# Fifteen Strassen pairs in the MLP instead of fourteen, with a new order of the last corners

## The reference

```python
ff = jnp.square(jax.nn.relu(x @ w_ff1)) @ w_ff2          # hidden width 4096
x  = layer_norm(ALPHA * x + ff, ln3_g, ln3_b)            # over the 1024 columns of a token
```

## Time and profile before

| | |
|---|---|
| median of 3 runs | 396.94 us (396.78 to 397.25) |
| the profiled execution | 396.8 us |
| its span, first to last instruction | 394.9 us |
| TensorE busy | 387.3 us (98%), 2090 matmuls |
| VectorE busy | 343.2 us (87%) |
| ScalarE busy | 258.5 us (65%) |
| POOL busy | 77.4 us (20%) |

### The profile page before, as it was taken

One profiled execution on the slowest core, in us unless ns is written; L12 is line 12 of the kernel. 1 busy time (PEld: TensorE's weight loads), 2 busy tenths in 40 slices (PEclk: granted clock), 3 DMA queues, 4 the chain that ended last, 5 costly groups with the idle time before them and its releaser, 6 DMA issues.

```text
span 394.9 us, 5646 instructions
## 1 busy us (share of the span) xinstructions
PE 387.3 (98%) x2090; PEld 331.7 (84%) x2090; DVE 343.2 (87%) x445; ACT 258.5 (65%) x344; POOL 77.4 (20%) x75
## 2 busy tenths in 40 slices
PE   8999999999999999999999999999999999999993
PEld 6888888888988888889988888888888888888882
DVE  5599595899988786969667899999999999999796
ACT  6666568756554638447645578777888888888720
POOL 2049400037870205000005300000000000000000
PEclk9999999999999999999999999999999999999999
DMA  8997737743656181563536449787677778776002
GB/s 292 373 378 269 248 107 250 259 159 113 224 195 215 63 300 65 212 214 116 205 135 209 135 145 305 218 245 227 210 242 217 230 234 243 231 235 218 0 2 106
DMA packets 25026, 79.44 MB, mean 201 GB/s; under 512 B 1735, under 2 KB 3111, under 8 KB 20903
## 3 DMA queue, kind: packets, MB, share of 16 engines
q1 hardware_dynamic: 22592, 75.24, 54.6%
q0 software_dynamic: 2016, 3.67, 5.4%
q10 hardware_dynamic: 390, 0.17, 0.2%
HBM read 78.02 MB, written 1.05 MB: 200 GB/s over the span
## 4 chain that ended last, share of the span: by engine, by line
PE 97%; DMA 1%; DVE 1%; issue 0%; DVEq 0%; ACT 0%
PE bank L1633 17%; PE bank L1634 17%; PE bank L1635 17%; PE bank L2018 13%; PE bank L1692 13%; PE bank L1696 7%; PE bank L2025 7%; PE bank L1844 2%; PE bank L1639 1%; DMA raw<-in_lead 1%; PE bank L1798 1%; PE bank L1831 0%; PE bank L1897 0%; PE bank L1946 0%; PE bank L1790 0%; PE bank L1789 0%
## 5 line engine op out<-in xcount | busy, mean ns | idle before, releaser
L1045 DVE TENSOR_TENSOR w_lo<-raw,w_hi 128x2048 fp32r<-128x2048 f32 x30 | 70.6, 2359 | 6.0 <-ACT w_hi L622 5.8
L622 ACT CAST w_hi<-raw 128x2048 fp32r<-128x2048 f32 x32 | 60.7, 1912 | 11.2 <-PE bank L1635 9.3
L2018 PE MATMUL bank<-actA,w_hi 128*128 128x512 f32 x224 | 55.4, 390 | 0.0
L2018 PEld LDWEIGHTS bank<-actA,w_hi 128*128 128x128 f32 x224 | 42.0, 188 | 8.7
L592 POOL DMA_DIRECT2D raw<-in_w_ff x14 | 12.3, 879 | 168.3 <-DMA raw<-in_w_ff 168.3
L1633 PE MATMUL bank<-w_hi,actB 128*128 128x512 f32 x107 | 42.6, 398 | 0.0
L1634 PE MATMUL bank<-w_lo,actB 128*128 128x512 f32 x107 | 41.8, 391 | 0.0
L1635 PE MATMUL bank<-w_hi,actB 128*128 128x512 f32 x107 | 41.7, 390 | 0.0
L1692 PE MATMUL bank<-actA,w_hi 128*128 128x512 f32 x156 | 38.3, 392 | 0.0
L1633 PE MATMUL bank<-w_hi,actA 128*128 128x512 f32 x96 | 38.0, 395 | 0.0
L1635 PE MATMUL bank<-w_hi,actA 128*128 128x512 f32 x96 | 37.4, 390 | 0.0
(11 more groups left out here) (243 smaller groups left out, 860.3 us busy)
## 6 DMA issues: line engine op xcount, KB each, us to landing
raw<-in_w_ff SPq DMA_DIRECT2D x32, 1024.0 KB, 5.3
raw<-in_w_in SPq DMA_DIRECT2D x10, 1024.0 KB, 7.1
raw<-in_w_xkv SPq DMA_DIRECT2D x8, 1024.0 KB, 5.0
raw<-in_w_mix_o SPq DMA_DIRECT2D x4, 1024.0 KB, 4.9
raw<-in_w_xq SPq DMA_DIRECT2D x4, 1024.0 KB, 5.0
raw<-in_w_xo SPq DMA_DIRECT2D x4, 1024.0 KB, 4.9
raw<-in_w_ff POOLq DMA_DIRECT2D x14, 256.0 KB, 5.0
raw<-in_lead SPq DMA_DIRECT2D x6, 384.0 KB, 5.0
```

Source lines behind the costliest of these rows:

```text
L622: act.copy(dst, half_view(u)).then_inc(hi_done, 1)
L1045: dve.tensor_tensor(dst, half_view(u), hi_part.bitcast(f32), ALU.subtract).then_inc(lo_done, 1)
L2018: pe.matmul(b[:, :].rearrange("p (h s) -> p h s", h=2), hi[:, k, m * P:(m + 1) * P], actA[:, :, k, :], start=k == 0, stop=False, skip_grou ...
```

## The change

`KINDS` gets a fifteenth S, so pair 14 is done with seven products and only pair 15 has eight. With it:

- TensorE's loop stops at pair 13, whose split around its second up block becomes 3 + 4; pair 14's seven products follow in one piece, and each corner then takes only pair 15's six matmuls, in the order P2, P3, P7, P4. Before, the order was both L pairs of the half 1 corners first, then of half 0.
- In ScalarE's and VectorE's last round pair 14 gets its sums. VectorE makes `add_halves` of pair 15 before `wsum_low` of pair 14 there. The low part of the last weight is one `up_low(16)` in the loop and no longer two half-width `last_weights_low`.
- `hidden_low` of pair 15 comes between the first and the second corner sum.
- P1's copy goes to `emptied` instead of the first quarter of `sums_w`, and waits for a relu (`relu_done`) instead of for `wsum_lo`.
- POOL issues one adding transfer more.

```diff
-KINDS = "SSSSSSSSSSSSSSLL"
+KINDS = "SSSSSSSSSSSSSSSL"
-        first_product, first_and_sixth, with_fifth, with_seventh = [sums_w[:, n * 512:(n + 1) * 512] for n in range(4)]
+        first_product = emptied[:, 0, :]
+        first_and_sixth, with_fifth, with_seventh = [sums_w[:, n * 512:(n + 1) * 512] for n in range(1, 4)]
...
-            down_high(LAST_S + 1)
-            empty(LAST_S + 2, 0)
-            up_high(PAIRS)
             square(LAST_S + 1)
-            hidden_high(LAST_S + 1)
-            act.wait_ge(wsum_lo, len(S_PAIRS))
+            act.wait_ge(relu_done, LAST_S - 1)
             act.wait_ge(product_done, 1)
             act.copy(first_product, bank[P_BANK["P1"]][:, :]).then_inc(p1_copied, 1)
-            empty(LAST_S + 2, 1)
-            square(LAST_S + 2)
-            hidden_high(LAST_S + 2)
+            hidden_high(LAST_S + 1)
...
-                wsum_low(q + 1)
-                add_halves(q + 2)
-            def last_weights_low(c):
...
-            down_low(LAST_S + 1)
-            last_weights_low(1)
-            hidden_low(LAST_S + 1)
-
+                if q == LAST_S - 1:
+                    add_halves(q + 2)
+                    wsum_low(q + 1)
+                else:
+                    wsum_low(q + 1)
+                    add_halves(q + 2)
...
             dve.tensor_tensor(b, b, first_product, ALU.add).then_inc(corner_done, 1)
-            add_halves(LAST_S + 2)
+            hidden_low(LAST_S + 1)
...
-            hidden_low(LAST_S + 2)
-            last_weights_low(0)
...
-            for q in range(1, LAST_S + 1):
-                order, cut = (ORDER, 4) if q < LAST_S else (LAST_ORDER, 2)
+            for q in range(1, LAST_S):
+                cut = 4 if q < LAST_S - 1 else 3
                 up_block(q + 2, 0)
-                multiply(q, order[:cut])
+                multiply(q, ORDER[:cut])
                 up_block(q + 2, 1)
-                multiply(q, order[cut:])
+                multiply(q, ORDER[cut:])
+            multiply(LAST_S, LAST_ORDER)
...
-            for n, q in [(0, PAIRS - 2), (1, PAIRS - 2), (0, PAIRS - 1), (1, PAIRS - 1), (2, PAIRS - 2),
-                         (3, PAIRS - 2), (2, PAIRS - 1), (3, PAIRS - 1)]:
-                corner(n, q)
+            for n in range(4):
+                corner(n)
```

More of the change, by code:

```diff
@@ L365, in build @@
         sq_done = sem("sq_done")
-        last_lo = sem("last_lo")
         up_hi, up_lo, up_full, up_free = map(sem, ("up_hi", "up_lo", "up_full", "up_free"))
@@ L2067, in _ @@
             multiply(0, FIRST_ORDER)
-            for q in range(1, LAST_S + 1):
-                order, cut = (ORDER, 4) if q < LAST_S else (LAST_ORDER, 2)
+            for q in range(1, LAST_S):
+                cut = 4 if q < LAST_S - 1 else 3
                 up_block(q + 2, 0)
-                multiply(q, order[:cut])
+                multiply(q, ORDER[:cut])
                 up_block(q + 2, 1)
-                multiply(q, order[cut:])
-            def corner(n, q):
+                multiply(q, ORDER[cut:])
@@ L2077, in corner @@
+            multiply(LAST_S, LAST_ORDER)
+            def corner(n):
                 name, t, c = [("P2", 1, 1), ("P3", 1, 0), ("P7", 0, 0), ("P4", 0, 1)][n]
                 pe.wait_ge(corner_done, n + 1)
[L2079 to L2084, removed]
+                pe.wait_ge(a_lo, PAIRS)
+                pe.wait_ge(up_lo, PAIRS - 1)
+                a = blocks[(PAIRS - 1) % 3]
@@ L2085, in corner @@
                 for m in range(2):
                     block_at = (2 * m + t) * P
[L2087 to L2091, removed]
-                    i = three(bank[P_BANK[name]][:, :], [a[:, at0 + block_at:at0 + block_at + P] for at0 in (0, 896)],
-                              mov, False, q == PAIRS - 1 and m == 1, on=True)
@@ L2094, in corner @@
-                if q == PAIRS - 1:
-                    i.then_inc(corner_full, 1)
-            for n, q in [(0, PAIRS - 2), (1, PAIRS - 2), (0, PAIRS - 1), (1, PAIRS - 1), (2, PAIRS - 2),
-                         (3, PAIRS - 2), (2, PAIRS - 1), (3, PAIRS - 1)]:
-                corner(n, q)
+                    mov = [v[:, 1, 0, m * 1024 + c * 512:m * 1024 + (c + 1) * 512] for v in (w_hi, w_lo)]
+                    i = three(bank[P_BANK[name]][:, :], [a[:, at0 + block_at:at0 + block_at + P] for at0 in (0, 896)],
+                              mov, False, m == 1, on=True)
@@ L2102 @@
+                i.then_inc(corner_full, 1)
+            for n in range(4):
+                corner(n)
 def kernel(**inputs):
```

## The result

The change made the kernel slower: 398.31 us median of 8 runs (398.08 to 398.67), against 396.95 for 8 runs of the kernel before (396.70 to 397.56). The ratio is 1.0031 (95% interval 1.0022 to 1.0039). The profiled execution took 398.31 with a span of 396.1.

The account below looks back on a forecast made before the run. TensorE (98% busy, 97% of the chain) bounded the kernel, with VectorE last after the change: 0.68 saved, 1.56 uncovered, +0.88 on 396.8 gives 397.7, 397.8 as a median. Range 397.3 to 398.5.

Parts of the forecast that it names:

- TensorE saves 0.68: From pair 13 on, TensorE has three matmuls less at 0.227 us each, so 0.68 us less work.
- The added round of sums fits: VectorE's and ScalarE's extra last round, sums for pair 14, ends in time for TensorE and is costed at nothing.
- The margins of 0.03 and 0.17: Spare us in the added round: 0.03 at hidden_low after ScalarE's copy, 0.17 from wsum_low's end to P6's weight load.
- rival (b): VectorE or ScalarE late in the added round, P6 waits, TensorE stalls 0.42 to 0.55: 398.2 to 398.4; 13%.
- The added transfer is hidden: POOL's fifteenth adding transfer lands by about 368.1 to 369, 1.7 to 2.6 us before ScalarE's copy at 370.70.
- Rival (c): Adding DMA comes after 370.7, holding up ScalarE's copy and VectorE's t2_sum; about 398.7 if a microsecond past its margin; 4%.
- The new home of P1's copy: ScalarE's copy of P1 needs only pair 14's relu done; gain at most 0.1 us, taken as nothing.
- VectorE's norm of half 1 sets the end, +0.88: At the end, 4.28 us of VectorE work no longer fits in 2.72: 1.56 uncovered against 0.68 saved; 70%.
- the lateness 1.56: VectorE's last bn_stats at 389.56 comes 1.56 us after TensorE delivers the last corner at 388.00.
- the forecast's own 397.5 to 398.1: Range for the main forecast alone, VectorE last and +0.88 us, given 70%.
- The rule of the most-contended engine: Skill's advice to optimize the highest-occupancy engine first; by it, TensorE's three fewer matmuls are worth their 0.68 us.
- the sum of 396.1: Rival (a): TensorE still releases the end, so 396.8 less 0.68 gives 396.1, as a median 396.26; 13%.

Follow-up runs that it names:

- The run with the old order: Changed kernel with wsum_low of pair 14 put back before add_halves of pair 15 in the last round: 399.27 us, ratio 1.0050.
- The idle matmuls: Changed kernel with six or thirteen extra unread matmuls on TensorE between second and third corner: 398.31 us (ratio 1.0027) and 399.35 us (1.0055).
- the removal of two operations: Changed kernel without VectorE's last two operations of half 1's norm (reciprocal root and shift): 396.90 us, ratio 0.9993.
- the repeat: The changed kernel measured once more, unaltered, on the same chip as its variants, against the kernel before: 398.22 us, ratio 1.0028.
- the kernel before with the shared norm: Kernel before, with half 1's scaling moved from VectorE to ScalarE and its shift to POOL: 397.78 us, ratio 1.0021.
- the run with the square root: Changed kernel, half 1's scaling on ScalarE and shift on POOL, half 0's root by ScalarE square root and VectorE reciprocal: 396.73 us, ratio 0.9989.

## Why the prediction was right

- **TensorE saves 0.68.** Right: 17.55 for 18.23 from pair 13's start to the last matmul, with no gap.
- **The added round of sums fits.** Right, step by step, each 0.29 to 0.33 after its forecast, of which 0.28 is the execution's late start: hidden_low at 375.49 (375.20 forecast), wsum_low 377.10 (376.81), first corner sum 379.50 (379.17), first bn_stats 384.68 (384.39). The margins of 0.03 and 0.17 held (wsum_low ended at 378.85, 0.16 before the weight load of P6's first matmul at 379.01), and rival (b) with its stall on P6 didn't happen. The run with the old order shows how little room the corner sums had: 1.30 us later there cost 0.96.
- **The added transfer is hidden.** Right: ScalarE's copy of pair 14's weights followed the empty before it at once (370.98 after 370.50; 0.49 in the earlier trace rows), with no wait, and POOL's last transfer was issued at 361.92, its transfers landing in 4.2 to 5.7. Rival (c) is out. The new home of P1's copy wasn't tried by itself; P1's copy waited 0.30 for TensorE, so its wait for the relu was no limit.
- **VectorE's norm of half 1 sets the end, +0.88.** Right in place and in size: bn_stats of half 1 at 385.56 (385.28 forecast), of half 0 at 389.24 (388.96), the lateness 1.56 as worked out, the span's median 0.9 longer. The idle matmuls (six free, thirteen not) and the removal of two operations (half 0's bn_stats 1.31 earlier, the span 1.1 shorter) show the cause from both sides.
- **What was mis-sized.** The sum put 0.88 on a time of 396.8, with the 1.9 us around the span taken as fixed. That step missed 0.3: the time around the span is 2.2 in the changed kernel. With the 0.9 of the span this gives 1.2; the rest up to the 1.36 between the medians is within their spread, since the repeat gave 1.07. The forecast of 397.8 was 0.5 too low. That is inside the stated range but outside the forecast's own 397.5 to 398.1, and inside rival (b)'s 398.2 to 398.4: the range held because it was drawn wide enough for (b), which is luck. By the time alone (b) would have seemed right; the timeline tells them apart.
- **The rule of the most-contended engine.** The prediction gave the rule's verdict to TensorE, by its 98%. Its work fell and the time rose, so for the last 8 us the trace disagrees with the sum of 396.1; for the body the chain (97% TensorE) agrees. The Trainium skill, Perfetto Trace Analysis, Identifying the Most-Contended Engine, would have TensorE judged by MFU (its arithmetic as a share of the peak) and by the share of its weight loads, and not by its matmuls. By weight loads TensorE stands at 84% in the earlier trace rows, so VectorE with its 87% was already ahead, which the prediction passed over. The same page of the Trainium skill (Optimization Strategy) remarks that the most-contended engine can change over time. The tail of the trace shows that.

## What to carry to other kernels

The end of a kernel is a race of its own: work taken off the engine with the highest share pays only down to the point where the next engine's closing chain is covered. Here the order of the last accumulations gave the other engine 5.44 us for 4.28 us of work, and the change halved that window while it saved 0.68. Before shortening the last stretch, count what the follower has to do between the last two results, and move that to an idle engine first; then look at what its outputs collide with.

## What the runs showed of the hardware that I had not expected

- The time of a run outside the profiled span is not fixed: 1.9 us with 445 VectorE instructions, 2.2 with 450, and it moved by 0.2 when only five one-element copies were added.
- Three stores of 256 KB that leave within a microsecond landed up to 2.5 us after their issue instead of 2.0; in the kernel before with the shared norm, 0.6 us more passed from VectorE's end to the end of the span than without it. In the run with the square root one of four took 2.5 too, though no three were issued within a microsecond, so what decides it stays open.
- The first matmuls of a run differ from run to run with nothing changed there: 3.67 to 4.18 us for the same six in the fourteen profiles.
